# Zeroed matmuls ahead of the first projections, other DMA times in the plan, other slots for the first up weights

## The reference, cut to what matters

```
h    = rmsnorm(x)                          # x: 2048 x 1024 per core
q, k, v, u = split(h @ w_in, 512 each)     # 8 heads of 64; u: 4 pooling groups of 128
y_attn = moba_attention(rope(q), rope(k), v)   # own 256-block, and the top 3 past blocks
y_pool = (trailing means of u - u) @ w_pool ...
x    = x + rmsnorm(concat(y_attn, y_pool) @ w_out)
a    = rmsnorm(x) @ w_up                   # 1024 -> 5632 = gate and value of 2816
a    = causal depthwise conv of width 3 over a
x    = x + rmsnorm((silu(gate) * value) @ w_down)
```

## Time and profile before

| | us |
|---|---|
| median of 3 runs | 788.35 (787.2 to 789.49) |
| the profiled execution, whole | 786.13 |
| its span, slowest core (core 3) | 784.6 |
| spans of the 8 cores | 781.5 to 784.6 |
| PE busy on core 3 | 747.5 (95%) |
| PE weight loads / DVE / ACT / POOL busy | 374.9 / 467.5 / 388.4 / 281.9 |
| chain that ended last: share on PE | 88% |

### The profile page before, as it was taken

The page is one execution under the profiler, slowest core; times in us unless marked ns, Lnnn a source line. Parts: engine busy times, 40 slices in busy tenths (PEclk is TensorE's granted clock), DMA queues, the critical chain, the costliest instruction groups (busy, mean ns, idle before and its releaser), DMA issues.

```text
span 784.6 us, 14577 instructions; the slowest of 8 cores (781.5 to 784.6 us)
## 1 busy us (share of the span) xinstructions
PE 747.5 (95%) x4724; PEld 374.9 (48%) x4724; DVE 467.5 (60%) x682; ACT 388.4 (50%) x629; POOL 281.9 (36%) x312
## 2 busy tenths in 40 slices
PE   2899899999999999999999999999999999999995
PEld 1375444556565664444444444444444444444442
DVE  4867766635464446677787772332777877872222
ACT  5476443578798997355554451111445444441111
POOL 1442452220334545366665562100343444330000
PEclk9999999999999999999999999999999999999999
DMA  8999982137349567949897657162444444002321
GB/s 257 312 260 255 167 166 71 42 35 124 102 117 214 150 184 137 192 94 195 157 197 131 119 105 113 55 213 109 108 81 81 71 70 77 1 0 80 109 81 54
DMA packets 65098, 99.72 MB, mean 127 GB/s; under 512 B 38016, under 2 KB 43904, under 8 KB 64000
## 3 DMA queue, kind: packets, MB, share of 16 engines
q1 hardware_dynamic: 52336, 66.01, 31.4%
q0 software_dynamic: 12688, 32.77, 25.6%
HBM read 100.99 MB, written 16.78 MB: 150 GB/s over the span
## 4 chain that ended last, share of the span: by engine, by line
PE 88%; DVE 3%; DMA 3%; issue 2%; ACT 2%; POOL 0%; SPq 0%; DVEq 0%; POOLq 0%; ACTq 0%
PE ps L879 37%; PE ps L962 19%; PE ps L773 8%; PE ps L831 7%; PE ps L708 6%; PE ps L613 5%; PE ps L791 4%; DMA MEM<-w_up_r 1%; PE ps L778 1%; DMA MEM<-x 1%; DMA MEM<-MEM 1%; DVE MEM L524 1%; DVE MEM L620 1%; PE ps L736 1%; SPq L160 0%
## 5 line engine op out<-in xcount | busy, mean ns | idle before, releaser
L879 PE MATMUL ps<-MEM 128*128 128x512 bf16 x1408 | 306.3, 379 | 2.8 <-DVE MEM L840 1.1
L879 PEld LDWEIGHTS ps<-MEM 128*128 128x128 bf16 x1408 | 137.2, 98 | 169.1 <-issue 5.4
L889 ACT ACTIVATE MEM<-ps,MEM 128x1024 f32<-128x1024 f32 x88 | 105.9, 1204 | 140.6 <-PE ps L879 138.0
L787 ACT ACTIVATE MEM<-ps 128x512 bf16<-128x512 f32 (+1 forms) x320 | 147.6, 544 | 33.8 <-PE ps L773 14.0
L962 PE MATMUL ps<-MEM 128*128 128x512 bf16 x704 | 152.3, 379 | 0.0
L915 POOL TENSOR_TENSOR MEM<-MEM 128x1024 bf16<-128x1024 f32 x44 | 103.4, 2351 | 124.2 <-DVE MEM L902 81.2
L892 DVE SCALAR_TENSOR_TENSOR MEM<-ps,MEM 128x1023 f32<-128x1023 f32 x88 | 112.7, 1282 | 51.9 <-ACT MEM L889 51.3
L895 DVE SCALAR_TENSOR_TENSOR MEM<-ps,MEM 128x1022 f32<-128x1022 f32 x88 | 112.6, 1280 | 8.0
L962 PEld LDWEIGHTS ps<-MEM 128*128 128x128 bf16 x704 | 68.9, 98 | 83.1
L773 PE MATMUL ps<-MEM 72*128 72x512 bf16 (+1 forms) x320 | 101.3, 348 | 4.1 <-DMA MEM<-MEM 2.0
L546 POOL TENSOR_SCALAR MEM<-MEM 128x1 f32<-128x1 f32 x63 | 12.1, 191 | 196.9 <-ACT MEM L970 118.8
(11 more groups left out here) (88 smaller groups left out, 586.5 us busy)
## 6 DMA issues: line engine op xcount, KB each, us to landing
MEM<-w_up_r POOLq DMA_DIRECT2D x44, 512.0 KB, 6.1
MEM<-x SPq DMA_DIRECT2D x32, 512.0 KB, 5.8
x1s<-MEM SPq DMA_DIRECT2D x16, 512.0 KB, 3.9
MEM<-x1s SPq DMA_DIRECT2D x16, 512.0 KB, 5.3
out<-MEM SPq DMA_DIRECT2D x15, 512.0 KB, 2.6
MEM<-w_down POOLq DMA_DIRECT2D x22, 256.0 KB, 7.3
MEM<-w_qk SPq DMA_DIRECT2D x4, 1024.0 KB, 14.8
MEM<-w_vu SPq DMA_DIRECT2D x4, 1024.0 KB, 20.7
```

What stands on the lines that cost most here:

```text
L787: op("act", lambda e, c0=c0, u=u, p=p: e.activation(out=PT[p][:, c0:512], in_=bk[u.ids[0]][:, c0:512], func=AF.Exp, scale=SCALE), rd=u.b, ...
L879: mm = op("pe", lambda e, c=c, half=half, pr=pr, ws=ws, tb=tb: e.matmul(bk[pr.ids[tb]], lhsT=wu[ws][:, c, half * 128:(half + 1) * 128], rh ...
L889: op("act", lambda e, pr=pr, ch=ch, ts=ts: e.activation(out=tA[ts], in_=ps(pr)[:, :], func=AF.Identity, scale=cwb[:, ch, 2:3], bias=cwb[:, ...
```

## The change

It has five parts.
1. A memset of the staging tile `stg[0][0]` on DVE and 60 matmuls on it, each 256 columns wide, into one PSUM bank. Their result is read by nobody. They have the worst `prio` of all, so the list scheduler puts them where PE has nothing else ready; their planned duration is that of 512 columns at full speed. The first use of `stg[0][0]` (L626 of the first unit) waits for all of them.
2. Planned DMA times: for transfers issued before 3 us a rate of 0.8 rather than 0.7 of RATE and a start of 2.2 rather than 3.0 us; on SP's line between 31 and 52 us a rate of 0.78 of what it was.
3. The up weight slots 0 and 1 lie in QT slot 0, slots 2 and 3 in the space of the pooling constants and the ring (and of the `diffs` tiles, whose readers are now waited for).
4. Units 0 and 1 of the first up section wait for the last matmul of `sec1(7)`.
5. In every unit the matmul (c=0, tb=1) waits for the one of (c=0, tb=0) (`lead`). PE runs its stream in order, so no semaphore is added; in the plan it keeps the second token half of a later unit from being placed ahead of its first half.

```diff
-                rate = self.CAST if o["cast"] else self.RATE * (0.7 if t < 3.0 else 1.0)
+                rate = self.CAST if o["cast"] else self.RATE * (0.8 if t < 3.0 else 1.0)
+                if e == "sp" and 31.0 < line[e] < 52.0:
+                    rate *= 0.78
...
-                    line[e] = max(line[e], t + (1.2 if t > 3.0 else 3.0)) + o["nbytes"] / (rate * (0.6 if busy else 1.0))
+                    line[e] = max(line[e], t + (1.2 if t > 3.0 else 2.2)) + o["nbytes"] / (rate * (0.6 if busy else 1.0))
...
-        wu = [b16v(a, 1024).rearrange("p (c n) -> p c n", c=8) for a in (aPL, aPL + 1024, aQT, aQT + 1024, aPT, aPT + 1024)]
+        wu = [b16v(a, 1024).rearrange("p (c n) -> p c n", c=8) for a in (aQT, aQT + 1024, aPL, aPL + 1024, aPT, aPT + 1024)]
...
+        zt, wk = stg[0][0], buf("stg0_0")
+        op("dve", lambda e: e.memset(f32v(aST, 256), 0.0), wr=[wk], n=256)
+        warm = Use(ALL8)
+        for i in range(60):
+            op("pe", lambda e: e.matmul(bk[warm.ids[0]][:, 0:256], lhsT=zt[:, 0:128], rhs=zt[:, 0:256], start=True, stop=True),
+               rd=[wk], n=512, **W(i == 0, warm.b[0]))["prio"] = 9000000 + i
...
+            sec_mm[tt] = mm
...
+                    lead = None
...
-                               deps=unit + (last_exp if 4 <= u < 8 else []) if c == tb == 0 else (),
+                               deps=unit + (last_exp if 4 <= u < 8 else []) + ([sec_mm[7]] if u < 2 else []) if c == tb == 0 else ([lead] if c == 0 else ()),
...
+                            lead = mm if c == tb == 0 else lead
...
-        wu_alias[0] = union(["poolc"])
-        wu_alias[1] = union(["ur%d" % i for i in range(5)])
+        wu_alias[2] = union(["poolc"])
+        wu_alias[3] = union(["ur%d" % i for i in range(5)] + ["df0", "df1"])
...
-        wu_alias[2] = wu_alias[3] = q_al[0]
+        wu_alias[0] = wu_alias[1] = q_al[0]
```

More of the change, by code:

```diff
@@ L824, in build @@
         last_sec = []
+        sec_mm = {}
         def sec1(tt):
```

## The result

| | before | after |
|---|---|---|
| median of 4 runs, us | 788.92 (787.2 to 791.01) | 797.81 (797.25 to 801.86) |
| ratio, 95% interval | | 1.0123 [1.0085, 1.0162] |
| span of the slowest core, us | 784.6 (core 3) | 796.5 (core 0) |
| PE busy on that core, us | 747.5 (95%) | 750.5 (94%) |

The change makes the kernel 1.2% slower. I had forecast 787.1 us and given 0.12 to anything slower.

A forecast was written before the change was run, and what follows sets the result against it. It took PE's long stream as the bound, its holes as the saving, and loads as an equal bound to 60 us. From 788.35, 1.2 off for the zeroed matmuls and 0 for the rest gave 787.1 us, range 783.8 to 790.6.

The forecast's parts named there:

- PSUM pairs (0,1) and (2,3) are free for those tiles, so I take 0: Up projection, hole ahead of unit 3: output projection of tiles 12 to 15 can fill it; 0 us, at worst +2.5.
- I take 0, nearest to the capped side: Planned DMA times reorder everything from 20 us on: 0 us, at worst one more hole with half clock, 2.6 us.
- Rival C: `lead` leaves PE idle at 314 us because tile 12's turned heads land late: 790.5 us, chance 0.16.
- 0.9 at each of units 4 to 7: Up projection hand-overs of bank pairs: 0.9 us lost at each of these units unless tiles 12 to 15 fill them.
- Part 1's 2.4 us: First two projection units: with the clock already up, 32 matmuls take 6.90 instead of 9.28 us, gaining 2.4 us.
- rival B: Kernel start: zeroed matmuls run out and the clock is down at 18.75 us, or the lead vanishes; 788.3 us, chance 0.17.
- 35% of 1.9 is 0.7 us; all of it is 1.9 ... I take 1.2: Share of the start's lead surviving to the end, from cores 1 and 6 up to group 2's gating: 1.2 us gained.
- The cap of 1.9 us: Last projection weights, cast from 44.99 us: transfers allow an end at 46.7 instead of 48.59, limiting the lead to 1.9 us.
- 4 matmuls a us: PE's pace on core 3 after the 2.02 us wait at 90 us, at a granted clock of 0.50.
- Rival A: The key and query DMA wait at 90 us shrinks and no core falls to half clock: 784.7 us, chance 0.24.
- Parts 3 and 4, 0: New up weight slots and the `sec1(7)` wait give 0 us; a 2.02 us hole at most if a load were late.

The follow-up runs named there:

- experiment 4: The kernel before with only `lead` added: 796.85 us, ratio 1.0106 to before.
- experiment 5: The kernel before with the zeroed matmuls, new up weight slots and `sec1(7)` wait, without planned DMA times and `lead`: 789.0 us, ratio 1.0009 to before.
- experiment 2: The changed kernel with tile 12's output projection held behind unit 9 and tiles 12 to 15 two pairs later: 787.92 us, ratio 1.000 to before.
- experiment 8: The kernel before with 72 zeroed matmuls, the last 32 of them 512 columns wide: 790.95 us, ratio 1.004 to before.
- experiment 1: The changed kernel with the up weight loads of pairs 4 and 5 issued only behind unit 3's last matmul: 785.78 us, ratio 0.997 to before.
- Experiment 10: The changed kernel with the weights of pairs 4 and 5 late and without memset and zeroed matmuls: 783.35 us, ratio 0.9948 to before.
- experiment 7: The changed kernel without the memset and the 60 zeroed matmuls: 798.89 us, ratio 1.014 to before.
- experiment 9: The kernel before with the up weight loads of pairs 4 and 5 behind unit 3's last matmul: 784.99 us, ratio 0.9976 to before.

## Why the prediction was wrong

**The failed step is Part 5's "PSUM pairs (0,1) and (2,3) are free for those tiles, so I take 0, range −2.8 to +2.5".** I asked whether the filler had a bank, and priced the case without it by the hole: 2.5 us, the time to unit 3's bank. But the filler was placed. Once a matmul stands in an in-order stream, PE waits for its data however late, and the hole's size is no bound: 4.45 to 13.02 us, with 1.3 us of half clock on the six matmuls alone. The bound to take was the landing of the last turned heads. No row that I read gave it; the trace of before has it, 12.3 to 15.2 us from issue to landing, with nobody behind it. On core 3 they landed at 321.9, 8.0 us after the end of unit 2 at 313.82. That bound would have been near, and still too small: in the changed kernel they take up to 23.8 us. In the change it is part 2 and not part 5 that places the filler; the wrong price is the same.

**Part 2's "I take 0, nearest to the capped side" failed with it.** Its price was that of a new order, and I bounded this by one more hole of 2.02 us, a wait that the trace had, 2.6 us with its half clock. It cost the whole loss, 9 to 10 us: experiments 4 and 5 put the six matmuls on part 2, whose plan has tile 12 ready in time because it counts 8.5 us for a landing of 15.4 to 23.8. A bound from the waits that an order has says nothing of the waits of another.

**Rival C** had nearly the place (314 us), the mechanism (tile 12 not ready, its last turned heads late) and the culprit row right, with a chance of 0.16. Its price was 3.4 us, the measured one 9 to 10. The place was one unit off in the change, ahead of unit 4 rather than of unit 3. It also named `lead` as the cause: sufficient on the kernel before, but in the change without effect on any stream. That part of it is refuted. "0.9 at each of units 4 to 7" was near: experiment 2 shows 1.03.

**Part 1's 2.4 us: rival B.** The projections ran at half clock again on 7 of 8 cores, as B said, and the time gained is none. B had PE run out of zeroed matmuls. On core 0, 11 were left at the gap of 2.22 us and stood behind the transposes that were late; by 15.8 us it had run out, and it idled 2.44 us ahead of the projection. That the idle time between the transposes matters, experiment 8 shows: with wide ones there the clock stays up on all cores. The Trainium skill's rule that transposes don't count as busy for the gate (TensorE: Matmul & The Clock Gate, Part 4, PE-mode transpose) is neither borne out nor refuted here, since the fall on core 0 follows plain idle time.

**"35% of 1.9 is 0.7 us; all of it is 1.9 ... I take 1.2"** was too much. Where the lead was really given (experiment 8) 0 reached the gating. The cores that I compared in the earlier trace rows differ in PE alone; the wait at 90 us is for a transfer whose time an earlier PE doesn't move, and a core that falls there pays for a half clock besides. The cap of 1.9 us was misread too. I took the cast at 44.99 for one that waits for its transfer; the row names no wait, and the last of these weights had landed on core 3 at 43.5. The last slices, those that PE waited for, stood behind a memset on DVE:

```profile
45.77 1.76 DVE L474 MEMSET MEM<- 8x2048 f32 x1 [0.48 <-DVE MEM L719]
47.57 0.88 DVE L524 TENSOR_SCALAR MEM<-MEM 128x256 bf16<-128x256 f32 x3
```

The "4 matmuls a us" of the earlier trace rows are no rate either: the x4 counts the records that touch this microsecond, and the seven of L708 behind it take 3.19 us.

That the zeroed matmuls cost something is possible, not shown: 1.0026 and 1.004, with intervals that begin at 0.9996 and 1.0001, and 0.997 against 0.9948 for experiments 1 and 10, whose intervals overlap; but the changed kernel without them (experiment 7) was not faster, 1.014 against 1.0123.

**Rival A happened and did not pay.** The wait at 90 us is gone on all cores of the changed kernel; from 60 to 100 us PE is busy for 39.60 us of 40 on core 0, for 37.12 before on core 3. But from 100 to 175 it is busy for 70.8 to 72.3 us on the eight cores, before for 73.3 to 74.0, and the up projection starts when it did before. Core 3 of the changed kernel also has a wait that no core had before, with a half clock behind it, and ends 3 to 5 us later than the others when the wait for the heads is taken off:

```profile
67.13 0.27 PE L744 MATMUL ps<-MEM 128*128 128x128 bf16 x2 [1.38 <-DMA MEM<-poolc]
```

Experiment 10, with 0.9948 against 0.9976 for the kernel before with the same cure, leaves room for a small gain from the new order, but the intervals overlap.

**Parts 3 and 4, 0:** part 4 had no effect on any stream, and with part 3 but without part 2 nothing was lost (experiment 5): pooling ends at 241.6 us there, and no weight load comes near 297. It is part 2's order that ends pooling at 296.2; part 3 then decides that the loads which wait for it are those of pairs 2 and 3 and not of 0 and 1. How much of the landing's lateness is due to them the runs bound: with pairs 4 and 5 out of the way the heads land after 5.5 to 6.7 us beside them (experiment 1), and after 3.8 to 4.9 us in the old order (experiment 9); beside pairs 4 and 5, after 15.4 to 23.8 us, and in the old order after 11.8 to 17.9 (before and experiment 4). The two orders differ in more than these loads, so this is argued, not shown.

## What to carry to other kernels

When a scheduler with planned times writes an in-order stream, price every filler by how late its data can land, not by the hole it fills; the row to read is the issue-to-landing time of the transfer it needs, even where nobody waits for it now, with room for a new order that loads the queues more (here 15.2 us became 23.8). A change to planned times alone is a change to every order: read the stream at each hand-over before costing it at nothing. And a warm start was worth here only what the next wait for a transfer let through.

## What the hardware showed that I had not expected

- The issue of a transposing DMA can hold SP for long: that of tile 11's input takes 9.9 to 14.7 us in the changed kernel, 3.7 to 5.9 before, and 1.2 to 1.8 when two weight loads are moved away. The landing of the one ahead of it, the last turned heads, goes from 5.5 to 6.7 us to 15.4 to 23.8.
- The busy share of the DMA engines did not tell the two apart: at 306 to 312 us on core 0 it is 1.09 with the loads and 1.12 without, while 205 and 269 GB/s are moved. From 310 to 330 us, with them, it is 1.06 and 1.18 at 176 and 120 GB/s.
- 40 zeroed matmuls in 6.54 us raised the clock, and behind one idle time of 2.22 us it was at 0.50 at 14 to 16 us, a stretch in which PE was busy for 2.00 of 2.00 us. Yet another core idled 2.02 us with 1.00 before and after.
